# Moving the tiles that TensorE reads: gaps of 32 to 384 bytes around the split weights, combined x and summed quarters

## The chip, the cores and the metric

The kernel runs on one core of a Trainium2 chip. The metric is the device time of one launch in microseconds (us), lower is better. The time before is the median of three runs: 3024.18 us (3021.7 to 3024.24).

## The reference, cut to what matters

The reference is a stack of two blocks over a sequence of 512 tokens with a width of 1024, all in float32. The first block has two layers, each with a fused input projection, retention, a state-space scan, forgetting attention and an output projection. The second has two layers, each of which is

```
x = layer_norm(ALPHA * x + 0.5 * swiglu(x, wg[0], wu[0], wd[0]))
x = layer_norm(ALPHA * x + token_mix(x, w_in, w_out, ...))
x = layer_norm(ALPHA * x + 0.5 * swiglu(x, wg[1], wu[1], wd[1]))
swiglu(x, wg, wu, wd) = (silu(x @ wg) * (x @ wu)) @ wd      # 1024 -> 2816 -> 1024
```

So there are four feed-forward halves, and beside them a row of projections from 1024 features.

## The kernel before, in words

**Products in two parts.** Every large product is made from operands that are split into a high part, rounded to float32r, and a low part, the rest. Three passes are added up in PSUM: high times high, high times low, low times high. A tile whose name ends in `_parts` holds both. Each matmul has a stationary operand of 128 x 128 (a weight load, PEld in the profile, goes ahead of the matmul) and a moving operand of 128 x 256 or 128 x 512. TensorE can load the next weights while the current matmul still streams.

**Tiles.** In each partition the persistent tiles lie in the order of their allocation, each at the next multiple of 32 bytes: `x_all`, `x_parts` (32,768 bytes, the activations), `w_raw`, `w_parts` (32,768 bytes: two slots, each with a high and a low part of 8,192 bytes), `cst` (3,796), `spec` (8,208), `par` (624), and behind them the tiles of the stages. In a feed-forward half these are `ffn_buffers`, `x_combined_parts` (32,768), `partial_parts` (8,192, two slots), `hidden_parts` (24,576) and `sum_parts` (24,576, two slots). Counted from the start of a partition, `x_parts` starts at byte 17,536, `w_parts` at 66,688, `x_combined_parts` at 137,280, `partial_parts` at 170,048, `hidden_parts` at 178,240 and `sum_parts` at 202,816.

**Weight units.** SP loads a unit of 8,192 bytes a partition into one of two slots of `w_raw`; ACT or DVE rounds it into the high part of the slot of `w_parts`, Pool or DVE makes the low part. In the projections this is `Stream` (`round`, `lower`), with the products in `Project` (L423 token by token, L347 and L425 with the weights as the moving operand). In the feed-forward halves it is `FeedForward.build`.

**A feed-forward half** goes through four `tile` units (L2212, moving 512 columns of `x_parts`), sixteen `quad` units, two more `tile` units and four `final` ones (L2293, moving `hidden_parts`; the last of them with 256 columns at L2304). A quad unit computes a 2 x 2 block product with seven multiplications (Winograd's form of Strassen's scheme), each 12 matmuls of 256 columns at L2250, in this order: a11 (`x_parts` against `w_parts`), s2 (`x_combined_parts` against `sum_parts`), s1 (`x_combined_parts` against `w_parts`), s3 (`x_combined_parts` against `sum_parts`), a12 (`x_parts` against `w_parts`), a22 (`x_combined_parts` against `w_parts`), s4 (`x_parts` against `sum_parts`). Behind s1 and behind a12 stands a partial product of the down projection (L2232: 12 matmuls of 512 columns, `hidden_parts` against `partial_parts`). Quads alternate: even ones are for the gate, odd ones for the up projection.

**The order of the work** is written out by hand on each engine. In a quad unit DVE does, in program order: the last combination of the quad before (L2542), the sums of the next unit's quarters (L2494 to L2501), one combination (L2523), the low part of the next unit (L2506), the low part of its sums (L2512), the addition of a partial product (L2555), and then L2528, for which PE waits ahead of a22:

```
pe.wait_ge(self.combined, 5 * q + 2)
multiply(a22, n4, 1, False)
```

Of the kernel before, what the change touches and what calls it, by code (L numbers as in the profile page):

```python
# [22 lines left out]
F32R = mybir.dt.float32r  # L23
# [5 lines left out]
T = 512  # L29
# [5 lines left out]
UNIT = KD * UC  # L35
SLOTS = 2
LOWERED = 512
HALF_TILE = P // 2
BIG = 1.0e30
EPS = 1e-6  # L40
LN_EPS = 1e-5
# [37 lines left out]
def split3(ap, a):  # L79
    return ap.rearrange("p (a b) -> p a b", a=a)  # L80
# [7 lines left out]
def repeat(ap, n):  # L88

    return ap.unsqueeze(1).broadcast_to([ap.shape[0], n, ap.shape[1]])  # L90


class Stream:
# [63 lines left out]
def build(nc, dr, out):  # L157
    ctx = ExitStack()
    with ctx:
        named = Counter()  # L160

        def sb(name, n, dt=F32, stack=None):
            named[name] += 1
            return (stack or ctx).enter_context(nc.sbuf_tensor(f"{name}{named[name] if named[name] > 1 else ''}", [P, n], dt))
# [53 lines left out]
        x_all = sb("x_all", KD * T)  # L218
        xs_all = sb("x_parts", 2 * KD * T, F32R)
        w_raw = sb("w_raw", SLOTS * UNIT)  # L220
        w_parts = sb("w_parts", 2 * SLOTS * UNIT, F32R)
        cst = sb("cst", C0N)
        spec = sb("spec", CN)
        par = sb("par", P1N)
        X = split3(x_all[:, :], KD)
        XS = xs_all[:, :].rearrange("p (a k t) -> p a k t", a=2, k=KD)
        RAW = split3(w_raw[:, :], SLOTS)
        WP = w_parts[:, :].rearrange("p (s a n) -> p s a n", s=SLOTS, a=2)
        ident = cst[:, 0:128]
        ones = cst[:, 128:256]  # L230
        triu = cst[:, 256:384]
# [49 lines left out]
        class Project:  # L281
# [20 lines left out]
            def both_parts(self, source):  # L302


                u = self.stream.add(source, KD * HALF_TILE, self.projected, len(self.jobs) + 1, turns=True)
                self.jobs.append((u, "b", 0, P, HALF_TILE, KD))
                return len(self.jobs) - 1
# [24 lines left out]
            def run_half(self, pe, j):  # L332
# [7 lines left out]
                if not second:  # L340
                    if self.jobs[j - c - 1][1] == "second":
                        pe.wait_ge(self.evacuated, j - c - 2 * NT + 2 * (c + 1))
                    elif c < 2:
                        pe.wait_ge(self.evacuated, j - 1)
                w = [WP[:, self.stream.slot(u), a, :].rearrange("p (k n) -> p k n", k=kt) for a in range(2)]
                def product(k, a, b, start, stop):
                    return pe.matmul(PS[:, self.bank(j), 0:m], XS[:, a, kt * second + k, c * P:(c + 1) * P], w[b][:, k, :],  # L347
                                     start=start and not second, stop=stop and second)
# [14 lines left out]
            def begin(self, pe, jobs, x, order=range(KD), between=None):  # L363
# [4 lines left out]
                for n in range(KD + 1):  # L368
                    if between and n in between:
                        between[n]()  # L370
                    if n < KD:
                        k = order[n]
                        pe.wait_ge(x.high, n + 1)
                        for j in jobs:
# [3 lines left out]
                            for a in range(2):  # L378
                                w = WP[:, self.stream.slot(u), a, 0:kt * ncols].rearrange("p (k n) -> p k n", k=kt)
                                pe.matmul(PS[0:m, self.bank(j), :], w[:, k, c:c + m], XS[:, 0, k, :],  # L380
                                          start=(n == 0 and a == 0), stop=False)
                    if n:
                        k = order[n - 1]
                        pe.wait_ge(x.low, n)
                        for j in jobs:
                            u, kind, c, m, ncols, kt = self.jobs[j]
                            w = WP[:, self.stream.slot(u), 0, 0:kt * ncols].rearrange("p (k n) -> p k n", k=kt)
                            last = pe.matmul(PS[0:m, self.bank(j), :], w[:, k, c:c + m], XS[:, 1, k, :],  # L388
# [4 lines left out]
            def run(self, pe, j, part, between=None):  # L393
# [16 lines left out]
                if kind == "b":  # L410
                    w = WP[:, self.stream.slot(u), 0, 0:kt * m].rearrange("p (k n) -> p k n", k=kt)
                    for k in range(kt):
# [6 lines left out]
                    return  # L419
                w = [WP[:, self.stream.slot(u), a, 0:kt * ncols].rearrange("p (k n) -> p k n", k=kt) for a in range(2)]  # L420
                def product(k, w_, x_, start, stop):
                    if kind == "f":
                        return pe.matmul(PS[0:m, self.bank(j), :], w[w_][:, k, c:c + m], part(x_, k),  # L423
                                         start=start, stop=stop)
                    return pe.matmul(PS[:, j % 2, 0:m], part(x_, k)[:, c * P:(c + 1) * P], w[w_][:, k, :],  # L425
                                     start=start, stop=stop)
# [16 lines left out]
            def after(self, j, act):  # L443

                u = self.jobs[j][0] if j >= 0 else -1
                if j + 1 == len(self.jobs) or self.jobs[j + 1][0] != u:
                    self.stream.round(act, act.copy, RAW, WP, u + 1 + SLOTS)

# [253 lines left out]
        first = ExitStack()  # L702
# [432 lines left out]
        def scan_and_attend(block, l, streams, norm, after):  # L1135
# [451 lines left out]
            def _(dve):  # L1587
# [6 lines left out]
                for h in range(2):  # L1594
                    norm_retention(h)
                dve.wait_ge(s_dt, 1)
                link(dve.tensor_tensor(dtf, split3(PS[:, 7, 0:96], NT), repeat(p1("dtf_b"), NT), ALU.add))
                dve.scalar_tensor_tensor(mag, dtf, -1.0, dtf, ALU.mult, ALU.max).then_inc(s_ab, 1)
                dve.wait_ge(s_ex, 1)
# [11 lines left out]
                                         ALU.min, ALU.subtract).then_inc(s_lf, 1)  # L1611
                dve.wait_ge(s_al, 1)
                dve.scalar_tensor_tensor(aa, dtf[:, :, 0:16], -1.0, repeat(amat, NT),
                                         ALU.mult, ALU.mult).then_inc(s_a, 1)

# [370 lines left out]
        HALF, QUARTER = T // 2, KD // 2 * P  # L1986
        SMALL = EARLY * P
# [10 lines left out]
        class FeedForward:  # L1998
# [78 lines left out]
            def build(self, block, before, after):  # L2077
                half, slot = self.half, self.slot
                ar = Arena(f"ffn{half}", 4 * T + 6 * HALF + 3 * QUARTER + 2 * SMALL)
# [2 lines left out]
                flat_sums = ar.take(3 * QUARTER)  # L2082
                sums = split3(flat_sums, 3)
                small_raw = split3(ar.take(2 * SMALL), 2)
                xt = ar.parts(f"x_combined_parts{half}", 8 * 4 * HALF).rearrange("p (a n k t) -> p a n k t", a=2, n=4, k=4)
                small_parts = ar.parts(f"partial_parts{half}", 4 * SMALL).rearrange("p (s a n) -> p s a n", s=2, a=2)
                hidden = ar.parts(f"hidden_parts{half}", 6 * 2 * T).rearrange("p (k a t) -> p k a t", k=6, a=2)
                early = ExitStack()
                xc = sb(f"x_combined{half}", 4 * 4 * HALF, stack=early)[:, :].rearrange("p (n k t) -> p n k t", n=4, k=4)
                early.close()  # L2090
                more = ar.parts(f"sum_parts{half}", 2 * 2 * 3 * QUARTER).rearrange("p (s a n) -> p s a n", s=2, a=2)
                ln = self.norm(f"ffn{half}_norm")
                passes = ((0, 0), (0, 1), (1, 0))
                units = range(NU)
# [1469 lines left out]
def constants():  # L3564
# [6 lines left out]
    c0[:, 256:384] = i[:, None] <= i[None, :]  # L3571
    c0[:, 768:896] = np.where(i[None, :] > i[:, None], -BIG, 0.0)
    c0[:, 896] = (10000.0 ** (-(i % 64) / 64.0)).astype(f)
# [19 lines left out]
    for q in range(NT):  # L3593
        ok = (np.arange(32)[None, :] * CS + CB - 1 <= (q * P + i)[:, None]) & (np.arange(32) < NCMP)[None, :]
        c2[:, 1536 + 32 * q:1568 + 32 * q] = np.where(ok, 0.0, -BIG)
        c2[:, 1664 + 32 * q:1696 + 32 * q] = ok
# [9 lines left out]
def layout(a):  # L3606

    def units(w, cols, n):

        L, K, _ = w.shape  # L3610
        w = w[:, :, cols].reshape(L, K // P, P, len(cols) // n, n)
        return np.ascontiguousarray(w.transpose(0, 3, 2, 1, 4)).reshape(L, len(cols) // n, P, -1)

    def padded(w, cols):

        w = np.concatenate([w[:, :, cols], np.zeros((DEPTH, D, HALF_TILE - len(cols)), np.float32)], axis=2)
        return units(w, np.arange(HALF_TILE), HALF_TILE)[:, 0]

# [88 lines left out]
```

## Time and profile before

| | |
|---|---|
| median of three runs | 3024.18 us |
| the profiled execution, first to last instruction (its span) | 3021.6 us |
| PE busy | 2964.2 us, 98% |
| weight loads (PEld) busy | 2512.2 us, 83% |
| DVE, ACT, POOL busy | 1899.1, 1289.1, 1072.1 us |
| mean granted TensorE clock | 0.990 |

The profile gives the profiled execution's time as its span alone; the lowest of the three timed runs, 3021.7 us, is as long. Times in the profile are in microseconds from the start of the span unless marked ns. PE is TensorE's matmuls, PEld its weight loads. Matmuls are pipelined, so that the duration of one reaches over the start of the next: how fast they run is seen from the distance of their starts. `L423` is line 423 of the kernel.

### The profile page before, as it was taken

Reading aid. Unit: us, or ns where it says so; the run is one execution under the profiler, and the core shown is the slowest. Engines: PE = TensorE matmul, PEld = TensorE weight load, DVE = VectorE, ACT = ScalarE, POOL = GpSimd, SP = SyncE. Lnnn points to the kernel's source line nnn. Section 1 sums busy time; section 2 is a strip of 40 time slices with the busy share of each in tenths; the row PEclk is TensorE's granted clock in tenths of the full one; section 3 lists DMA queues with packets and bytes.
Section 4 is the critical chain, followed back from the end, with each engine's and each line's share of the span. In section 5 each row is a group of like instructions: output and inputs, shape, how many; then the busy total and the mean of one; then the engine's idle time right before and its main releaser. Section 6 shows DMA issues by size and latency. Waiting matters only on the chain. (4 is left out here: it accounts for less than half of the span.)

```text
span 3021.6 us, 43644 instructions
## 1 busy us (share of the span) xinstructions
PE 2964.2 (98%) x17620; PEld 2512.2 (83%) x17620; DVE 1899.1 (63%) x2758; ACT 1289.1 (43%) x2015; POOL 1072.1 (35%) x786
## 2 busy tenths in 40 slices
PE   8999999999999999999999999999999999999998
PEld 6887878788778799988767899988998776789996
DVE  8476245747524377855386778657785537677875
ACT  4356442436553243424463534334343346453432
POOL 2443445535353422225342322242222534132222
PEclk8999999999999999999999999999999999999999
DMA  6223315313231233322110323223332221033321
GB/s 275 101 85 112 101 51 198 138 59 127 83 122 37 88 114 105 105 85 89 67 43 29 111 99 105 98 78 118 102 103 83 92 70 43 29 105 105 102 101 49
DMA packets 57440, 287.61 MB, mean 95 GB/s; under 512 B 6777, under 2 KB 7289, under 8 KB 30201
## 3 DMA queue, kind: packets, MB, share of 16 engines
q1 hardware_dynamic: 54000, 269.30, 25.3%
q10 hardware_dynamic: 3240, 15.53, 1.6%
q8 instruction: 140, 2.29, 0.3%
q14 instruction: 60, 0.48, 0.1%
HBM read 282.64 MB, written 2.16 MB: 94 GB/s over the span
## 5 line engine op out<-in xcount | busy, mean ns | idle before, releaser
L152 POOL TENSOR_TENSOR w_parts<-w_raw,w_parts 128x512 fp32r<-128x512 f32 x376 | 537.7, 1460 | 687.0 <-ACT w_parts L141 664.3
L423 PE MATMUL PS<-x_parts,w_parts 128*128 128x512 f32 x2640 | 655.1, 394 | 1.6 <-ACT m_all L1430 1.6
L423 PEld LDWEIGHTS PS<-x_parts,w_parts 128*128 128x128 f32 x2640 | 490.7, 188 | 111.3 <-issue 9.6
L2191 POOL TENSOR_TENSOR partial_parts<-ffn_buffers,partial_parts 128x512 fp32r<-128x512 f32 x128 | 183.0, 1431 | 747.6 <-ACT partial_parts L2398 747.6
L2232 PE MATMUL PS<-hidden_parts,partial_parts 128*128 128x512 f32 x1536 | 372.7, 391 | 0.0
L2232 PEld LDWEIGHTS PS<-hidden_parts,partial_parts 128*128 128x128 f32 x1536 | 280.1, 188 | 53.3
L2212 PE MATMUL PS<-x_parts,w_parts 128*128 128x512 f32 x1152 | 265.9, 392 | 3.1 <-POOL x_parts L1977 3.1
L2212 PEld LDWEIGHTS PS<-x_parts,w_parts 128*128 128x128 f32 x1152 | 215.9, 188 | 52.1 <-POOL x_parts L1977 4.5
L141 ACT CAST w_parts<-w_raw 128x2048 fp32r<-128x2048 f32 (+1 forms) x92 | 170.6, 1854 | 163.1 <-PE PS L423 73.8
L2250 PE MATMUL PS<-x_parts,w_parts 128*128 128x256 f32 x1536 | 204.3, 282 | 0.0
L2250 PE MATMUL PS<-x_combined_parts,w_parts 128*128 128x256 f32 x1536 | 204.0, 282 | 0.0
L2250 PE MATMUL PS<-x_combined_parts,sum_parts 128*128 128x256 f32 x1536 | 203.0, 281 | 0.0
L2250 PEld LDWEIGHTS PS<-x_combined_parts,sum_parts 128*128 128x128 f32 x1536 | 195.9, 190 | 5.0
L2250 PEld LDWEIGHTS PS<-x_combined_parts,w_parts 128*128 128x128 f32 x1536 | 191.6, 189 | 10.1 <-DVE ffn_buffers L2528 7.4
L2398 ACT CAST partial_parts<-ffn_buffers 128x512 fp32r<-128x512 f32 x128 | 79.2, 621 | 270.5 <-PE PS L2232 270.5
L2250 PEld LDWEIGHTS PS<-x_parts,w_parts 128*128 128x128 f32 x1536 | 192.4, 190 | 0.3
L347 PE MATMUL PS<-w_parts,x_parts 128*128 128x512 f32 x768 | 185.4, 399 | 1.4 <-ACT ssd_buffers L1468 1.4
L347 PEld LDWEIGHTS PS<-w_parts,x_parts 128*128 128x128 f32 x768 | 143.8, 188 | 38.3 <-issue 7.2
L2388 ACT CAST w_parts<-w_raw 128x2048 fp32r<-128x2048 f32 x64 | 122.5, 1915 | 88.2 <-DVE w_raw L2496 87.4
L2506 DVE TENSOR_TENSOR w_parts<-w_raw,w_parts 128x2048 fp32r<-128x2048 f32 x64 | 146.7, 2292 | 17.4 <-ACT w_parts L2388 17.4
L2378 ACT CAST hidden_parts<-ffn_buffers 128x512 fp32r<-128x512 f32 x88 | 54.6, 621 | 220.0 <-DVE ffn_buffers L2548 119.2
L2512 DVE TENSOR_TENSOR sum_parts<-ffn_buffers,sum_parts 128x1536 fp32r<-128x1536 f32 x64 | 148.3, 2318 | 0.0
(445 smaller groups left out, 5008.0 us busy)
## 6 DMA issues: line engine op xcount, KB each, us to landing
w_raw<-in_w_gu SPq DMA_DIRECT2D x88, 1024.0 KB, 4.8
w_raw<-in_w_in SPq DMA_DIRECT2D x70, 1024.0 KB, 4.9
ffn_buffers<-in_w_part SPq DMA_DIRECT2D x128, 256.0 KB, 2.7
w_raw<-in_w_out SPq DMA_DIRECT2D x24, 1024.0 KB, 4.8
m_all<-in_w_next SPq DMA_DIRECT2D x14, 1024.0 KB, 7.7
w_raw<-in_w_last SPq DMA_DIRECT2D x12, 768.0 KB, 4.1
m_all<-in_w_gate SPq DMA_DIRECT2D x8, 1024.0 KB, 5.0
ssd_buffers<-decay_rows ACTq DMA_DIRECT2D x16, 512.0 KB, 4.0
```

The source lines that it names most:

```text
L141: op(self.part(parts, u, 0, 0, n), raw[:, self.slot(u), 0:n]).then_inc(self.high, 1)
L152: pool.tensor_tensor(self.part(parts, u, 1, at, to), raw[:, self.slot(u), at:to], self.part(parts, u, 0, at, to).bitcast(F32), ALU.subtrac ...
L347: return pe.matmul(PS[:, self.bank(j), 0:m], XS[:, a, kt * second + k, c * P:(c + 1) * P], w[b][:, k, :], start=start and not second, stop ...
L423: return pe.matmul(PS[0:m, self.bank(j), :], w[w_][:, k, c:c + m], part(x_, k), start=start, stop=stop)
L2191: pool.tensor_tensor(small_parts[:, d % 2, 1, :], small_raw[:, d % 2, :], small_parts[:, d % 2, 0, :].bitcast(F32), ALU.subtract).then_inc ...
L2212: return pe.matmul(PS[:, 2 * b + g, :], WP[:, slot(b), w, c:c + P], XS[:, x, k, :], start=start, stop=stop)
L2232: last = pe.matmul(PS[:, 6 + d % 2, :], small_parts[:, d % 2, w, k * P:(k + 1) * P], hid(x, EARLY * c + k), start=(i == j == 0), stop=(i = ...
L2250: last = pe.matmul(bank(q, n), w(wa, k), x(xa, k), start=(first and k == 0 and i == 0), stop=(k == 3 and i == 2), skip_group_check=True)
L2388: act.copy(WP[:, b, 0, :], RAW[:, b, :]).then_inc(self.wide, 1)
L2398: act.copy(small_parts[:, d % 2, 0, :], small_raw[:, d % 2, :]).then_inc(self.small_high, 1)
L2506: dve.tensor_tensor(WP[:, b, 1, :], RAW[:, b, :], WP[:, b, 0, :].bitcast(F32), ALU.subtract).then_inc(self.sums, 1)
L2512: dve.tensor_tensor(split3(more[:, b, 1, :], 3), sums, split3(more[:, b, 0, :], 3).bitcast(F32), ALU.subtract).then_inc(self.sums, 1)
```

## The change

`w_parts` is allocated with 96 elements (384 bytes) ahead of its first slot and 48 elements (192 bytes) behind each slot. `x_combined_parts` begins 8 elements (32 bytes) later in its tile, `partial_parts` has 16 elements (64 bytes) behind each of its slots, and `sum_parts` 40 elements (160 bytes) behind each; `hidden_parts` has no gap. The larger tiles move what is allocated behind them: everything behind `w_parts` starts 768 bytes later, `partial_parts` 800, `hidden_parts` and `sum_parts` 928. `x_parts` and what lies before it stay. No instruction, wait or order changes.

```diff
+FIRST_GAP, SLOT_GAP = 96, 48
+PART_GAPS = dict(x_combined=(8, 0), partial=(0, 16), hidden=(0, 0), sums=(0, 40))
...
+def slots_of(ap, gap, n):
+
+    return ap.rearrange("p (s r) -> p s r", s=2)[:, :, 0:n].rearrange("p s (a n) -> p s a n", a=2)
...
-        w_parts = sb("w_parts", 2 * SLOTS * UNIT, F32R)
+        w_parts = sb("w_parts", FIRST_GAP + SLOTS * (2 * UNIT + SLOT_GAP), F32R)
...
-        WP = w_parts[:, :].rearrange("p (s a n) -> p s a n", s=SLOTS, a=2)
+        WP = slots_of(w_parts[:, FIRST_GAP:], SLOT_GAP, 2 * UNIT)
...
-                xt = ar.parts(f"x_combined_parts{half}", 8 * 4 * HALF).rearrange("p (a n k t) -> p a n k t", a=2, n=4, k=4)
-                small_parts = ar.parts(f"partial_parts{half}", 4 * SMALL).rearrange("p (s a n) -> p s a n", s=2, a=2)
-                hidden = ar.parts(f"hidden_parts{half}", 6 * 2 * T).rearrange("p (k a t) -> p k a t", k=6, a=2)
+                def parts_behind_gap(name, n):
+                    first, between = PART_GAPS[name]
+                    return ar.parts(f"{name}_parts{half}", first + n + 2 * between)[:, first:], between
+
+                xt = parts_behind_gap("x_combined", 8 * 4 * HALF)[0].rearrange("p (a n k t) -> p a n k t", a=2, n=4, k=4)
+                small_parts = slots_of(*parts_behind_gap("partial", 4 * SMALL), 2 * SMALL)
+                hidden = parts_behind_gap("hidden", 6 * 2 * T)[0].rearrange("p (k a t) -> p k a t", k=6, a=2)
...
-                more = ar.parts(f"sum_parts{half}", 2 * 2 * 3 * QUARTER).rearrange("p (s a n) -> p s a n", s=2, a=2)
+                more = slots_of(*parts_behind_gap("sums", 2 * 2 * 3 * QUARTER), 2 * 3 * QUARTER)
```

## Rows read from the trace of the kernel before

**Rows 1.** The page's part 1: busy us, share of the span, instructions, by engine.

```profile
PE 2964.2 (98%) x17620; PEld 2512.2 (83%) x17620; DVE 1899.1 (63%) x2758; ACT 1289.1 (43%) x2015; POOL 1072.1 (35%) x786
```

**Rows 2.** Span and mean granted TensorE clock of the core.

```profile
core 0: 3021.6 us, clock 0.990
```

**Rows 3.** PE groups by form: count, busy us, mean ns; idle before, releaser.

```profile
L423 PE MATMUL PS<-x_parts,w_parts 128*128 128x512 f32 x2640 | 655.1, 394 | 1.6 <-ACT m_all L1430 1.6
L2232 PE MATMUL PS<-hidden_parts,partial_parts 128*128 128x512 f32 x1536 | 372.7, 391 | 0.0
L2212 PE MATMUL PS<-x_parts,w_parts 128*128 128x512 f32 x1152 | 265.9, 392 | 3.1 <-POOL x_parts L1977 3.1
L2250 PE MATMUL PS<-x_parts,w_parts 128*128 128x256 f32 x1536 | 204.3, 282 | 0.0
...
L347 PE MATMUL PS<-w_parts,x_parts 128*128 128x512 f32 x768 | 185.4, 399 | 1.4 <-ACT ssd_buffers L1468 1.4
L2293 PE MATMUL PS<-hidden_parts,w_parts 128*128 128x512 f32 x432 | 103.8, 399 | 0.0
L425 PE MATMUL PS<-w_parts,x_parts 128*128 128x256 f32 x768 | 101.2, 291 | 1.6 <-POOL w_parts L152 1.4
...
L2304 PE MATMUL PS<-hidden_parts,sum_parts 128*128 128x256 f32 x144 | 17.9, 283 | 0.0
```

**Rows 4.** Timeline of PE, 50 to 190: start, length, group, count.

```profile
53.85 54.56 PE L423 MATMUL PS<-x_parts,w_parts 128*128 128x512 f32 x240
108.25 23.19 PE L425 MATMUL PS<-w_parts,x_parts 128*128 128x256 f32 x192
131.28 0.82 PE L1016 MATMUL PS<-cst,retention_buffers 128*128 128x128 f32 x6
```

**Rows 5.** Timeline of PE in the final units of a half, 1350 to 1392.

```profile
1350.75 12.76 PE L2293 MATMUL PS<-hidden_parts,w_parts 128*128 128x512 f32 x54
1363.35 1.02 PE L1804 MATMUL PS<-x_all,cst 128*128 128x512 f32 x2
...
1381.74 4.48 PE L2304 MATMUL PS<-hidden_parts,sum_parts 128*128 128x256 f32 x36
1386.06 0.95 PE L1814 MATMUL PS<-cst,ffn_buffers 128*128 128x1 f32 x8
```

**Rows 6.** Timeline of PE: a first quad's a22; an even and an odd quad.

```profile
1094.14 1.58 PE L2250 MATMUL PS<-x_combined_parts,w_parts 128*128 128x256 f32 x12
...
1143.34 1.59 PE L2250 MATMUL PS<-x_parts,w_parts 128*128 128x256 f32 x12
...
1155.96 1.67 PE L2250 MATMUL PS<-x_combined_parts,w_parts 128*128 128x256 f32 x12
1157.47 1.53 PE L2250 MATMUL PS<-x_parts,sum_parts 128*128 128x256 f32 x12
1158.83 1.60 PE L2250 MATMUL PS<-x_parts,w_parts 128*128 128x256 f32 x12
1160.27 1.58 PE L2250 MATMUL PS<-x_combined_parts,sum_parts 128*128 128x256 f32 x12
...
1171.46 1.58 PE L2250 MATMUL PS<-x_combined_parts,w_parts 128*128 128x256 f32 x12
1172.87 1.58 PE L2250 MATMUL PS<-x_parts,sum_parts 128*128 128x256 f32 x12
1174.29 1.60 PE L2250 MATMUL PS<-x_parts,w_parts 128*128 128x256 f32 x12
```

**Rows 7.** Timeline of DVE in the same quads: the chain's head, and L2528.

```profile
1093.14 0.41 DVE L2528 TENSOR_TENSOR ffn_buffers<-PS,ffn_buffers 128x256 f32<-128x256 f32 x1
...
1143.54 0.42 DVE L2542 TENSOR_TENSOR ffn_buffers<-ffn_buffers,PS 128x256 f32<-128x256 f32 x1 [0.19 <-PE PS L2250]
...
1155.50 0.41 DVE L2528 TENSOR_TENSOR ffn_buffers<-PS,ffn_buffers 128x256 f32<-128x256 f32 x1
...
1167.48 0.42 DVE L2528 TENSOR_TENSOR ffn_buffers<-PS,ffn_buffers 128x256 f32<-128x256 f32 x1
```

## The prediction

> **What bounds the kernel now.** I read the busy shares first. TensorE (PE) is busy 2964.2 of 3021.6 us, 98%, DVE 63%, ACT 43% [rows 1], and its granted clock averages 0.990 of the 2.4 GHz level [rows 2]. So nearly all of the time is matmuls in a row, and what counts is how far apart their starts are. The change touches no instruction, no wait, no queue and no shape: it only moves tiles. It can act on the time only if the start-to-start distance of matmuls depends on where their two operands lie.
>
> The mean durations of the groups [rows 3] don't show that, because a matmul is pipelined and its duration (some 282 ns for 256 columns, 391 to 399 ns for 512) overlaps the next. The timeline does: take the start of one run, the start of the next, and divide by the count.
> - 512 columns, x_parts against w_parts: (108.25 - 53.85) / 240 = 226.7 ns [rows 4].
> - 256 columns, w_parts against x_parts: (131.28 - 108.25) / 192 = 119.9 ns [rows 4].
> - 512 columns, hidden_parts against w_parts: (1363.35 - 1350.75) / 54 = 233.3 ns, with no idle time shown [rows 5].
> - 256 columns, hidden_parts against sum_parts: (1386.06 - 1381.74) / 36 = 120.0 ns [rows 5].
> - 256 columns inside the quad units: x_parts/w_parts (1160.27 - 1158.83) / 12 = 120 ns; x_parts/sum_parts once (1158.83 - 1157.47) / 12 = 113.3 ns and once (1174.29 - 1172.87) / 12 = 118.3 ns [rows 6].
>
> So one shape has two or three speeds, and the slow one of 512 columns has other tiles than the fast one. The lowest, 113.3 and 226.7, I call the floor. The last pair has the same tiles at two speeds: the fast one stands behind a matmul run that began with a wait, so how the weight load and the moving read stand to each other in time matters beside the address.
>
> The distance in bytes from the moving tile to the stationary one, modulo 512 (the step between two 128-column weight blocks), follows from the order of allocation and the sizes. Before: x_parts/w_parts 0; x_combined/sum_parts 0; hidden/partial 0; hidden/sum_parts 0; x_combined/w_parts 64; hidden/w_parts 64; x_parts/sum_parts 448 (64 the other way). With rows: at distance 0 the 256-column form is at its slowest (120), the 512-column one at the floor; at 64 the 512-column form is slow (233.3); at 448 the 256-column form has 118.3 or 113.3.
>
> **The change, part by part.** After it the distances (slot 0, slot 1) are: x_parts/w_parts 384, 64 (576); x_combined/w_parts 160, 352; x_combined/sum_parts 128, 288; x_parts/sum_parts 352, 0; hidden/partial 384, 448; hidden/w_parts 32, 224; hidden/sum_parts 0, 160. Nearly every pair leaves its old distance, and no row shows what most of the new ones cost. So each form is bounded from both sides by the rows of its shape.
>
> (a) Quad units, 84 matmuls of 256 columns and 24 of 512 each; 64 units, 16 in each of four feed-forward halves (1536 + 1536 + 1536 + 768 matmuls of L2250 and 1536 of L2232; the first group and L2232 stand in [rows 3]). An odd unit lasts 1174.29 - 1158.83 = 15.46 us [rows 6]; at the floor 84 x 0.1133 + 24 x 0.2267 = 14.96. Bounds for an odd unit: 0.50 us saved, or, with all 256-column matmuls at 120 (now 118.7 on average: (15.46 - 24 x 0.2287) / 84, with 228.7 for the 512s, halfway between floor and what two steps above it would give), 0.11 lost. I take the middle between 113.3 and 120, 116.7, as both ends are seen at the present distances and the new ones lie between: 84 x 2.0 ns = 0.17, and 0.02 for the 512s: 0.19 us a unit.
>
> What hides it: in an even unit the a22 products wait for DVE. L2528 ends at 1155.50 + 0.41 = 1155.91 and they start at 1155.96; the DVE work before it began at 1143.54, 0.20 behind the unit's start at 1143.34, and is a chain of its own [rows 6, 7]. A PE that is faster in the first 60 + 24 matmuls arrives earlier and waits longer; behind the wait it runs at 113.3 already. So even units give nothing (7 of 8; 28 in all). In an odd unit L2528 ends at 1167.90 against a start of a22 at 1171.46, 3.56 us of room; in the first unit of a half 1093.55 against 1094.14, 0.59 [rows 6, 7], more than the 0.36 that a floor-fast first part could save. So 32 odd and 4 first units count: 36 x 0.19 = 6.8 us (bounds: -4 to +18).
>
> (b) The other 256-column forms, L425 768 and L2304 144 [rows 3], from 119.9 to 116.7: 912 x 3.3 ns = 3.0 us (bounds 0 to 6.0).
>
> (c) L2293, 432 matmuls at 233.3 [rows 3, 5], distance 64 to 32 and 224: halfway to the floor, 432 x 3.3 = 1.4 us (0 to 2.9).
>
> (d) The 512-column x_parts/w_parts forms: L423 2640, L2212 1152, L347 768, together 4560 [rows 3], at the floor [rows 4]. They can't gain. I take 0; the other end is the 6.6 ns of L2293: 30 us lost. I take 0 because the slow 512-column row has w_parts, too, but a moving tile that starts 64 bytes off a 128-byte boundary, while x_parts stays where it is, on one; that is weak, and is the first rival.
>
> (e) Everything behind w_parts moves by 768 bytes or more (constants, buffers, par). ACT, DVE and Pool work on them, and have room (63% and less) except in the even units, where DVE's 12.4 us chain sets the a22 start. I take its durations as unchanged; 1% on it would be 0.12 x 28 = 3.5 us either way. DMA sizes and issues are the same: nothing.
>
> Sum: 6.8 + 3.0 + 1.4 = 11.2 us, made against the profiled execution's span of 3021.6. The median of the runs is 3024.18, 2.6 us above the span (0.09%); I put the saving under the median: 3024.2 - 11.2 = 3013.
>
> The Trainium skill, "SBUF — State Buffer", section "Who interferes with whom", says that PE has two SBUF read ports, one for the moving operand and one for the weight load, and never waits on anyone; by this rule no address could matter and the time would stay at 3024. The trace disagrees with it in this kernel: 226.7 against 233.3 ns for one shape with no wait shown [rows 4, 5].
>
> **The rivals.**
> 1. Slower: the 512-column forms leave the one distance at which they are known to be at the floor. Slot 1 of w_parts gets distance 64 to x_parts, the very distance of the 233.3 ns row [rows 5]. Half of 4560 times 6.6 ns = 15.0 us lost, against 11.2 gained: 3028. With slot 0 as bad: 3043. It decides from 11.2 / 4560 = 2.5 ns a matmul on. For it: the only slow 512-column row is the one at a distance of 64. Against it: at 64 and 448 the 256-column forms are faster than at 0, and L2293's moving tile is another.
> 2. Large gain: the new distances keep all forms at the floor, as x_parts/sum_parts at 1157.47 [rows 6]. 36 x 0.50 + 6.0 + 2.9 = 27 us: 2997. Against it: the same pair is at 118.3 in the unit beside.
> 3. No change: the speeds come from the rhythm of the instruction pairs (the entry behind a wait), not the address; all shifts are multiples of 32 bytes. 3024. For it: 113.3 and 118.3 at one distance [rows 6]. Against it: 226.7 against 233.3.
>
> **How the numbers follow.** Forecast 0.47, large gain 0.16, no change 0.13, slower 0.24. A difference under 0.2%, 6 us, can't be told from none. Faster: 0.16 + 0.46 (0.01 of the forecast's chance lies within 6 us) = 0.62; same 0.14; slower 0.24. The range is 2994 to 3034: it takes in the large gain and the milder slower case, with the 3.5 us of (e) on either side and a little for the pricing of rival 1, and leaves out both slots slow (3043). The likeliest case alone has 3004 to 3018.
>
> **What would show it.** Right: the run of L425 (192 matmuls in 23.03 us) gets shorter, towards 22.4; the run of L423 (240 in 54.40) stays; odd units fall below 15.46 and even ones stay near 15.49 with L2528's end still just before a22. Slower rival: L423's run grows beyond 55.0. Large gain: L425's run at 21.8 and odd units at 15.0. No change: every one of these stays. The prediction is wrong if L423 moves, or if even units shorten (then DVE's chain was not the limit).

## The result, and the profile after

The changed kernel takes 3046.2 us (median of 4 runs, 3042.4 to 3047.5) where the kernel before takes 3023.8 us (4 runs, 3021.7 to 3024.2). The ratio is 1.0075, 95% interval 1.006 to 1.009: slower by 0.75%, or 22 us. The forecast was 3013 us, faster by 11 us; the time also lies outside the range of 2994 to 3034.

The page of the profile after, its head and part 1 (busy us, share, instructions by engine), and under it the core's span and clock:

```profile
span 3045.3 us, 43644 instructions
PE 2989.2 (98%) x17620; PEld 2512.0 (82%) x17620; DVE 1899.2 (62%) x2758; ACT 1288.1 (42%) x2015; POOL 1066.9 (35%) x786
```

```profile
core 0: 3045.3 us, clock 0.991
```

The span grew by 23.7 us, PE's busy time by 25.0, with the same 17620 matmuls; DVE and ACT have what they had, Pool 5 us less, and the clock is 0.991 for 0.990 [rows 1, 2]. So the loss is in how closely the matmuls follow one another. Line numbers are 7 to 11 higher than before (L423 is now L430, L425 L432, L347 L354, L2212 L2223, L2232 L2243, L2250 L2261, L2293 L2304, L2304 L2315, L2528 L2539), and the tile `sum_parts` is called `sums_parts`.

PE groups by form after: count, busy us, mean ns, idle before. They answer to [rows 3]:

```profile
L430 PE MATMUL PS<-x_parts,w_parts 128*128 128x512 f32 x2640 | 666.7, 398 | 1.6 <-ACT m_all L1437 1.6
L2243 PE MATMUL PS<-hidden_parts,partial_parts 128*128 128x512 f32 x1536 | 376.1, 393 | 0.0
L2223 PE MATMUL PS<-x_parts,w_parts 128*128 128x512 f32 x1152 | 271.9, 396 | 4.3 <-POOL x_parts L1984 3.5 <-POOL x_parts L873 0.7
L2261 PE MATMUL PS<-x_parts,w_parts 128*128 128x256 f32 x1536 | 199.8, 279 | 0.0
...
L354 PE MATMUL PS<-w_parts,x_parts 128*128 128x512 f32 x768 | 187.9, 402 | 1.3 <-ACT ssd_buffers L1475 1.3
L2304 PE MATMUL PS<-hidden_parts,w_parts 128*128 128x512 f32 x432 | 103.8, 399 | 0.0
L432 PE MATMUL PS<-w_parts,x_parts 128*128 128x256 f32 x768 | 97.3, 284 | 1.5 <-POOL w_parts L159 1.5
```

The 512-column forms lose: 655.1 to 666.7, 265.9 to 271.9, 372.7 to 376.1, 185.4 to 187.9. The 256-column forms with `w_parts` and `x_parts` gain: 204.3 to 199.8 and 101.2 to 97.3. Busy time counts the union of overlapping instructions, so I also summed the start-to-start distances over all matmuls of either trace: `x_parts`/`w_parts` in 512 columns +21.1 us, `w_parts`/`x_parts` in 512 columns +2.3, `hidden_parts`/`partial_parts` +4.8, `x_combined_parts`/`w_parts` +1.1, `x_parts`/`sums_parts` +1.4, the matmuls of unsplit float32 +1.4; the 256-column `x_parts`/`w_parts` -4.6 and `w_parts`/`x_parts` -3.9. That is 23.6 of the span's 23.7.

Only about 1 us of the last term is speed. The rest is two stretches of the token-mixing stage in which the 24 matmuls stood further apart before. Timeline of PE in one of them, before, and then in e1_parts_only, the first experiment below, whose distance for this pair is as before:

```profile
2413.86 4.64 PE L425 MATMUL PS<-w_parts,x_parts 128*128 128x256 f32 x24
2418.34 0.97 PE L2831 MATMUL PS<-cst,mixer_buffers 112*128 112x24 f32 x8
```

```profile
2420.08 3.13 PE L432 MATMUL PS<-w_parts,x_parts 128*128 128x256 f32 x24
2423.04 0.97 PE L2842 MATMUL PS<-cst,mixer_buffers 112*128 112x24 f32 x8
```

The 24 matmuls take 4.48 us before and 2.96 in e1 (and 2.96 in the changed kernel). In all, the pair's matmuls lose 3.0 us in e1 too, so these 3 us don't come from the pair's distance. What held them apart isn't shown.

Timeline of PE after, the runs of [rows 4] and [rows 5]: start, length, group, count:

```profile
54.59 56.06 PE L430 MATMUL PS<-x_parts,w_parts 128*128 128x512 f32 x240
110.49 22.87 PE L432 MATMUL PS<-w_parts,x_parts 128*128 128x256 f32 x192
133.19 0.82 PE L1023 MATMUL PS<-cst,retention_buffers 128*128 128x128 f32 x6
...
1362.53 12.76 PE L2304 MATMUL PS<-hidden_parts,w_parts 128*128 128x512 f32 x54
1375.12 1.02 PE L1811 MATMUL PS<-x_all,cst 128*128 128x512 f32 x2
```

The run of 240 takes 110.49 - 54.59 = 55.90 us, 232.9 ns a matmul, where it took 54.40, 226.7 ns: the forecast's own sign of the slower rival ("beyond 55.0"). The run of 192 takes 22.70 us, 118.2 ns, from 119.9. The run of 54 takes 12.59, from 12.60: unchanged at 233.1 ns.

Timeline of PE after, an even and an odd quad unit, for [rows 6]; then DVE's L2539, the last thing that a22 waits for, for [rows 7]:

```profile
1154.46 1.58 PE L2261 MATMUL PS<-x_parts,w_parts 128*128 128x256 f32 x12
...
1167.12 1.60 PE L2261 MATMUL PS<-x_combined_parts,w_parts 128*128 128x256 f32 x12
1168.56 1.57 PE L2261 MATMUL PS<-x_parts,sums_parts 128*128 128x256 f32 x12
1169.97 1.52 PE L2261 MATMUL PS<-x_parts,w_parts 128*128 128x256 f32 x12
1171.33 1.58 PE L2261 MATMUL PS<-x_combined_parts,sums_parts 128*128 128x256 f32 x12
...
1185.33 1.58 PE L2261 MATMUL PS<-x_parts,w_parts 128*128 128x256 f32 x12
```

```profile
1166.32 0.41 DVE L2539 TENSOR_TENSOR ffn_buffers<-PS,ffn_buffers 128x256 f32<-128x256 f32 x1
...
1178.56 0.42 DVE L2539 TENSOR_TENSOR ffn_buffers<-PS,ffn_buffers 128x256 f32<-128x256 f32 x1
```

The even unit takes 15.51 us, the odd one 15.36. In this even unit a22 starts 0.39 us behind L2539's end (1166.73), so here PE itself comes late; in 3 of the 28 even units that aren't the first of a half the gap is 0.40, in 11 some 0.1, in 14 0.06, where all 28 had 0.06 before. Over all four halves even units average 15.565 us (15.480 before), odd ones 15.453 (15.459 before).

### The profile page after: what moved, and what is told of

It reads as the page before. It is cut to its first block and busy times, and to the rows that moved or that the text cites. A ratio compares the mean times of both kernels' runs of the same rounds, so it can differ in the third digit from the quotient of the medians.

```text
span 3045.3 us, 43644 instructions
## 1 busy us (share of the span) xinstructions
PE 2989.2 (98%) x17620; PEld 2512.0 (82%) x17620; DVE 1899.2 (62%) x2758; ACT 1288.1 (42%) x2015; POOL 1066.9 (35%) x786
## 5 line engine op out<-in xcount | busy, mean ns | idle before, releaser
L430 PE MATMUL PS<-x_parts,w_parts 128*128 128x512 f32 x2640 | 666.7, 398 | 1.6 <-ACT m_all L1437 1.6
L430 PEld LDWEIGHTS PS<-x_parts,w_parts 128*128 128x128 f32 x2640 | 491.4, 188 | 121.7 <-issue 9.6
L2243 PE MATMUL PS<-hidden_parts,partial_parts 128*128 128x512 f32 x1536 | 376.1, 393 | 0.0
L2243 PEld LDWEIGHTS PS<-hidden_parts,partial_parts 128*128 128x128 f32 x1536 | 280.0, 188 | 55.3
L2223 PE MATMUL PS<-x_parts,w_parts 128*128 128x512 f32 x1152 | 271.9, 396 | 4.3 <-POOL x_parts L1984 3.5
L2223 PEld LDWEIGHTS PS<-x_parts,w_parts 128*128 128x128 f32 x1152 | 215.7, 188 | 59.3 <-POOL x_parts L1984 4.3
L2261 PE MATMUL PS<-x_combined_parts,w_parts 128*128 128x256 f32 x1536 | 204.9, 282 | 0.0
L2261 PE MATMUL PS<-x_combined_parts,sums_parts 128*128 128x256 f32 x1536 | 202.6, 281 | 0.0
L2261 PEld LDWEIGHTS PS<-x_combined_parts,w_parts 128*128 128x128 f32 x1536 | 193.2, 188 | 11.2 <-DVE ffn_buffers L2539 7.8
L2261 PE MATMUL PS<-x_parts,w_parts 128*128 128x256 f32 x1536 | 199.8, 279 | 0.0
L2261 PEld LDWEIGHTS PS<-x_combined_parts,sums_parts 128*128 128x128 f32 x1536 | 195.1, 188 | 5.5
L354 PE MATMUL PS<-w_parts,x_parts 128*128 128x512 f32 x768 | 187.9, 402 | 1.3 <-ACT ssd_buffers L1475 1.3
L2261 PEld LDWEIGHTS PS<-x_parts,w_parts 128*128 128x128 f32 x1536 | 188.7, 188 | 0.3
L354 PEld LDWEIGHTS PS<-w_parts,x_parts 128*128 128x128 f32 x768 | 144.1, 188 | 40.5 <-issue 7.2
L2523 DVE TENSOR_TENSOR sums_parts<-ffn_buffers,sums_parts 128x1536 fp32r<-128x1536 f32 x64 | 148.4, 2318 | 0.0
```

Of the source, the lines that this page charges most:

```text
L2223: return pe.matmul(PS[:, 2 * b + g, :], WP[:, slot(b), w, c:c + P], XS[:, x, k, :], start=start, stop=stop)
L2243: last = pe.matmul(PS[:, 6 + d % 2, :], small_parts[:, d % 2, w, k * P:(k + 1) * P], hid(x, EARLY * c + k), start=(i == j == 0), stop=(i = ...
L2261: last = pe.matmul(bank(q, n), w(wa, k), x(xa, k), start=(first and k == 0 and i == 0), stop=(k == 3 and i == 2), skip_group_check=True)
L2523: dve.tensor_tensor(split3(more[:, b, 1, :], 3), sums, split3(more[:, b, 0, :], 3).bitcast(F32), ALU.subtract).then_inc(self.sums, 1)
```

## The experiments

All are edits of the changed kernel's constants unless a longer diff stands. "Distance" is the bytes from the moving to the stationary tile, modulo 512, as in the prediction. The 1.0 of each ratio is the kernel before, measured beside the runs (3023.3 us beside the e runs, 3024.2 beside the f runs, 3023.2 beside the g runs).

### Halves of the change: the tiles behind, or w_parts

e1_parts_only keeps the gaps of the three feed-forward tiles and takes those of `w_parts` away:

```diff
-FIRST_GAP, SLOT_GAP = 96, 48
+FIRST_GAP, SLOT_GAP = 0, 0
```

> Theory D (the speed of a matmul goes by the distance from the moving to the stationary tile modulo 512; the 512-column form has its floor of 226.7 ns only at 0): w_parts back at distance 0 to x_parts brings the 512-column forms of x_parts and w_parts back to 226.7 (the run of 240 back to 54.40 us); hidden_parts against partial_parts keeps 384 and 448 and stays at about 232 and 230. About 3024 + 5 = 3029 us (3025 to 3032). Rival Q (the gaps inside the quad units carry the loss): stays near 3040 or above. Rival A (not the distance but the moved addresses of what lies behind w_parts, worked on by DVE, ACT and Pool): 160 to 480 bytes remain, some loss spread over all engines, 3030 to 3046, with DVE and ACT groups of longer mean duration.

e2_w_only is the other half:

```diff
-PART_GAPS = dict(x_combined=(8, 0), partial=(0, 16), hidden=(0, 0), sums=(0, 40))
+PART_GAPS = dict(x_combined=(0, 0), partial=(0, 0), hidden=(0, 0), sums=(0, 0))
```

> Theory D: the 512-column forms of x_parts and w_parts at distance 384 and 64 take about 232 to 233 ns, some 23 us more than before; the 256-column x_parts/w_parts and w_parts/x_parts forms gain about 8 us; hidden_parts against partial_parts is back at distance 0: 3038 to 3042 us. Rival Q: about 3024, as the quad tiles are not moved against each other. Rival A: 3046, as everything behind w_parts is moved by 768 bytes as in the changed kernel.

Measured: e1 3026.4 us, ratio 1.0012 [1.0003, 1.0022]; e2 3041.5 us, 1.006 [1.0045, 1.0075]. Timeline of PE, first e1, then e2:

```profile
57.42 54.56 PE L430 MATMUL PS<-x_parts,w_parts 128*128 128x512 f32 x240
111.82 23.19 PE L432 MATMUL PS<-w_parts,x_parts 128*128 128x256 f32 x192
134.85 0.82 PE L1023 MATMUL PS<-cst,retention_buffers 128*128 128x128 f32 x6
```

```profile
54.53 56.07 PE L430 MATMUL PS<-x_parts,w_parts 128*128 128x512 f32 x240
110.44 22.87 PE L432 MATMUL PS<-w_parts,x_parts 128*128 128x256 f32 x192
133.14 0.82 PE L1023 MATMUL PS<-cst,retention_buffers 128*128 128x128 f32 x6
```

In e1 both runs are those of before to 0.01 us (54.40, 23.03); in e2 both are those of after (55.91, 22.70). So the move of `w_parts` makes both, and costs about 18 us. The other gaps cost about 3: in e1 the group `hidden_parts`/`partial_parts`, which left distance 0 for 384 and 448, is busy 375.7 us against 372.7 [rows 3], and in e2, where both tiles moved together, 372.0.

### Is it the distance, and modulo what?

e3_first512 moves `w_parts` and all behind it by 512 bytes; e4_first64 by 64:

```diff
-FIRST_GAP, SLOT_GAP = 96, 48
+FIRST_GAP, SLOT_GAP = 128, 0
```

> Only a first gap of 512 bytes: w_parts and everything behind it moves by 512 bytes, and every distance modulo 512 is as before. Theory D: each form keeps its speed and the time is that of before, 3024 us within 0.1%. Rival A (moved addresses cost by themselves): slower, 3035 to 3046. If the distance counts modulo more than 512 (1024 or 2048), the run of 240 moves away from 54.40 us.

```diff
-FIRST_GAP, SLOT_GAP = 96, 48
+FIRST_GAP, SLOT_GAP = 16, 0
```

> Only a first gap of 64 bytes: x_parts/w_parts goes from distance 0 to 64 in both slots, x_parts/sum_parts from 448 to 0, all other distances stay. Theory D: 512-column x_parts/w_parts 233 ns instead of 226.7 (the run of 240: 55.9 us), about 5040 matmuls, +30 us; the 256-column x_parts/w_parts matmuls of the quads fall from 119.7 to about 114.5, -4 us where PE sets the time, and w_parts/x_parts at L432 to 117.8, -2 us: 3046 to 3050 us. Rival A: a move of 64 bytes costs a twelfth of 768: within 0.1% of 3024.

(Both also have PART_GAPS at zero, as in e2.) Measured: e3 3023.6 us, ratio 1.0000 [0.9991, 1.001]; e4 3041.7 us, 1.006 [1.0045, 1.0075]. Timeline of PE in e3, then in e4:

```profile
53.76 54.56 PE L430 MATMUL PS<-x_parts,w_parts 128*128 128x512 f32 x240
108.16 23.19 PE L432 MATMUL PS<-w_parts,x_parts 128*128 128x256 f32 x192
131.19 0.82 PE L1023 MATMUL PS<-cst,retention_buffers 128*128 128x128 f32 x6
```

```profile
53.80 56.16 PE L430 MATMUL PS<-x_parts,w_parts 128*128 128x512 f32 x240
109.80 22.77 PE L432 MATMUL PS<-w_parts,x_parts 128*128 128x256 f32 x192
132.41 0.82 PE L1023 MATMUL PS<-cst,retention_buffers 128*128 128x128 f32 x6
```

e3 moves everything that the change moves and leaves every distance as it was modulo 512: no effect. So a move of the constants, buffers or weights costs nothing by itself, and it is not a distance modulo more than 512. A shorter period isn't excluded. At distances 256 apart the 512-column matmuls are equally fast (128 and 384: 232.5 and 232.5 ns; 192 and 448: 229.1 and 229.5; 160 and 416: 233.5 and 233.4), so that modulo 256 fits these rows as well; modulo 128 doesn't (64 and 192: 233.3 and 229.1).

e4 leaves the pairs behind `w_parts` to each other as they were, gives `x_parts`/`w_parts` 64 and takes `x_parts`/`sums_parts` from 448 to 0: 56.00 us for the run of 240 (233.3 ns), 22.61 for the run of 192 (117.8). The 233.3 is what I expected; the whole came 4 us or more below what I expected. The sums of the start-to-start distances say why: the 512-column matmuls with `x_parts` and `w_parts` lost 24.6 us and not 30 (23.1 as `x_parts`/`w_parts`, 5.4 ns each, and 1.4 as `w_parts`/`x_parts`, which lies at 448 when the other way round is 64, and has 229.6 ns there). The 256-column forms gained 4.7 us together, 3 of them in the two stretches of the token-mixing stage.

### The other direction: 512 columns to distance 0, 256 columns off it

If that is the rule, tiles can be placed by it. f1_hidden64 leaves `w_parts` alone and starts `partial_parts` and what lies behind it 64 bytes later. That brings `hidden_parts`/`w_parts` from 64 to 0, `x_combined_parts`/`sums_parts` from 0 to 64, `x_parts`/`sums_parts` from 448 to 0, and leaves `hidden_parts`/`partial_parts` at 0 and `x_combined_parts`/`w_parts` at 64:

```diff
-FIRST_GAP, SLOT_GAP = 96, 48
-PART_GAPS = dict(x_combined=(8, 0), partial=(0, 16), hidden=(0, 0), sums=(0, 40))
+FIRST_GAP, SLOT_GAP = 0, 0
+PART_GAPS = dict(x_combined=(0, 0), partial=(16, 0), hidden=(0, 0), sums=(0, 0))
```

> w_parts without gaps, partial_parts, hidden_parts and sum_parts 64 bytes later: every 512-column pair is at distance 0 (hidden_parts/w_parts comes from 64 to 0), x_combined/sum_parts goes to 64, x_parts/sum_parts to 0. Theory D (distance modulo 512 sets the speed, 512 columns want 0): the run of 54 at L2304 falls from 12.60 to 12.24 us (226.7 ns), 432 x 6.6 ns = 2.9 us saved, x_parts/sum_parts at 120 costs up to 2 us, x_combined/sum_parts between 113.3 and 117.7: 3019 to 3023 us. Rival B (the last tile's speed goes by its place on a 128-byte boundary, not by the distance): hidden_parts is now on a 128-byte boundary as well, so this run alone can't tell B from D for it; B expects x_combined/sum_parts, whose moving tile stays off the boundary, to stay at 118.5.

Measured: 3016.5 us, ratio 0.9975 [0.9965, 0.9985], faster than the 3019 to 3023 that I expected. Timeline of PE in f1, the run of 54 of [rows 5]:

```profile
1351.23 12.40 PE L2304 MATMUL PS<-hidden_parts,w_parts 128*128 128x512 f32 x54
1363.47 1.02 PE L1811 MATMUL PS<-x_all,cst 128*128 128x512 f32 x2
```

12.24 us, 226.7 ns: the form that took 230 to 234 ns in every kernel up to here is at the floor as soon as its distance is 0, with the same tiles and the same instructions. It gives 2.6 us (the group's busy time 103.8 to 101.2), and `x_combined_parts`/`sums_parts` 3.5 (203.0 to 199.5). `x_combined_parts`/`w_parts` gives 3.7 (204.0 to 200.3) although its distance of 64 is unchanged: behind s2 it now steps at 113.3 ns, where it had 117.8, and no wait stands ahead. `x_parts`/`sums_parts` loses 2.3 (99.6 to 101.9).

One tile can't lie at 0 for the 512-column forms and elsewhere for the 256-column ones, so f3_split gives the quads' weights their own offset in the slot of `w_parts`, 64 bytes in, and places the rest so that all 256-column pairs of the quads have distance 64 and all 512-column pairs 0, except the 72 matmuls of `hidden_parts`/`sums_parts`, which get 64 (233.3 ns):

```diff
+FIRST_GAP, SLOT_GAP = 0, 128
+QUAD_SHIFT, TOKEN_SHIFT = 16, 112
+PART_GAPS = dict(x_combined=(16, 0), partial=(0, 0), hidden=(0, 0), sums=(16, 0))
...
+        WQ = w_shifted(QUAD_SHIFT)
...
-                        act.copy(WP[:, b, 0, :], RAW[:, b, :]).then_inc(self.wide, 1)
+                        act.copy(WQ[:, b, 0, :], RAW[:, b, :]).then_inc(self.wide, 1)
```

(DVE's low part and PE's `kept_quarters` read and write `WQ` in the same way; `w_shifted(n)` is the view of the two slots from element n on.)

> The quad units write and read their weights 64 bytes further in the slot than all other units; x_combined, partial_parts and hidden_parts 64 bytes later, sum_parts 128. So all 256-column pairs of the quads are at distance 64 and all 512-column pairs at 0 (hidden/sum_parts at 64). Theory D: 512-column forms at their floor, quads at 113.3 to 117.7 ns; an odd quad unit between 15.0 and 15.35 us instead of 15.46, even ones near 15.49 (DVE's chain holds them); 36 x 0.1 to 0.45 us + 2.9 us = 3005 to 3018 us. Rival P (inside a distance the rhythm decides, 117.7 is the lock unless a wait stands before): 3015 to 3018.

f4_quad_only is f3 without the gaps of the other tiles (PART_GAPS zero): only the quads' weights move, by 64 bytes.

> Only the quad units' weights lie 64 bytes further in their slot, all tiles else keep their distances: x_parts/w_parts in the quads 64, x_combined/w_parts 128, x_combined/sum_parts 0, x_parts/sum_parts 448. Theory D: 512-column forms unchanged; of the quads' pairs one better (64), one worse (128, 118.5 to 119): 3019 to 3024 us, worse than f3_split by at least 4 us. Rival P (x_parts/w_parts decides alone, as in slot 1 of the changed kernel): as fast as f3_split without its 2.9 us.

f5_split_tokens is f3 with the units of the 256-column projections (L425 before) moved in their slot as well, by 448 bytes, which brings their distance from 0 to 64:

```diff
-        WQ = w_shifted(QUAD_SHIFT)
+        WQ, WT = w_shifted(QUAD_SHIFT), w_shifted(TOKEN_SHIFT)
...
+                self.stream.shifted[u] = WT
```

> f3_split, and the units whose weights are the moving operand of 256 columns at L432 lie 448 bytes further in their slot, which puts x_parts at distance 64 from them instead of 0. Theory D, with 64 as the good distance for 256 columns: the run of 192 falls from 23.03 us to 21.8 to 22.6; 768 matmuls, 2 to 5 us below f3_split. Rival B (the boundary of 128 bytes): the moving tile is off the boundary now, so no gain.

g3_split192 is f3 with 192 in place of 64 for all four 256-column pairs of the quads:

```diff
-QUAD_SHIFT, TOKEN_SHIFT = 16, 112
-PART_GAPS = dict(x_combined=(16, 0), partial=(0, 0), hidden=(0, 0), sums=(16, 0))
+QUAD_SHIFT, TOKEN_SHIFT = 48, 112
+PART_GAPS = dict(x_combined=(16, 0), partial=(0, 0), hidden=(0, 0), sums=(48, 0))
```

> f3_split with distance 192 instead of 64 for all 256-column pairs of the quads. Theory D in its strict form (64 is the good distance, all others but 0 are alike at 118 to 119): odd units 15.43 instead of 15.33, 3018 to 3021 us. Rival (192 is as good or better, as x_combined/w_parts at 192 had 115.4 in e2_w_only): odd units at or below 15.33, 3012 to 3017 us.

| | median us | ratio [95%] | odd units, us | even units, us |
|---|---|---|---|---|
| before | 3023.8 | 1 | 15.459 | 15.480 |
| after | 3046.2 | 1.0075 [1.006, 1.009] | 15.453 | 15.565 |
| f1 | 3016.5 | 0.9975 [0.9965, 0.9985] | 15.353 | 15.527 |
| f3 | 3016.7 | 0.9975 [0.9965, 0.9985] | 15.328 | 15.518 |
| f4 | 3023.1 | 0.9996 [0.9987, 1.0004] | 15.373 | 15.572 |
| f5 | 3012.9 | 0.9963 [0.9951, 0.9976] | 15.322 | 15.511 |
| g3 | 3015.4 | 0.9977 [0.9967, 0.9987] | 15.316 | 15.525 |

f5 against f3 changes one pair only, 768 matmuls. The medians are 3.8 us apart, with intervals that overlap; by the traces 2.1 us of it are this pair's, and the rest lies in groups that the step doesn't touch. PE's timeline in f5 has

```profile
53.39 54.56 PE L438 MATMUL PS<-x_parts,w_parts 128*128 128x512 f32 x240
107.79 22.78 PE L440 MATMUL PS<-w_parts,x_parts 128*128 128x256 f32 x192
130.41 0.82 PE L1031 MATMUL PS<-cst,retention_buffers 128*128 128x128 f32 x6
```

22.62 us for the run of 192 (117.8 ns) and 54.40 for the run of 240: the gain of the change at L425 without its loss at L423. f4, where only the quads' weights moved (`x_parts`/`w_parts` 64, `x_combined_parts`/`w_parts` 128, the other pairs as before), gives nothing that can be told: its odd units gain 0.09 us, its even ones lose as much. f3 came out at the slow end of what I expected, and no faster than f1: its 256-column forms go mostly at 117.8 ns, not at the floor, although `x_parts`/`w_parts` at the same distance of 64 goes at 114.1 in f4. g3 refutes my expectation that only 64 is good: at 192 the quads are as fast as at 64 (the intervals overlap). f5 beats the kernel before by 0.37% and the changed one by 33 us; only g1, which is f5 with one more step, is level with it.

### The wait for DVE in even units

The last two experiments move no tile. g1_split_order is f5 with one step of DVE's program order moved in even quads: the addition of the first partial product goes behind `lower_right` and the combination that a22 waits for. g2_order_only does the same to the kernel before.

```diff
-                        if beside:
+                        late = q is not None and q % 2 == 0
+                        if beside and not late:
...
+                            if beside and late:
+                                add_partial(beside[0])
```

> f5_split_tokens, and in even quad units DVE does the combination that a22 waits for ahead of the addition of the partial product (0.68 us), not behind it. Theory C (DVE's chain is what keeps the even units from gaining by faster matmuls): its end moves 0.7 us ahead, the wait before a22 goes, even units fall from 15.51 us to the 15.32 of the odd ones: 28 x 0.19 = 5.3 us, 3006 to 3009 us. Rival (something else holds the even units, or the wait's good rhythm of 113.3 ns behind it is worth as much as the wait costs): even units stay at 15.5 and the time near 3013.

> The same change of DVE's order without any shift (all distances as before). Theory C: the wait of some 100 ns ahead of a22 goes, but the 24 matmuls behind it then run at 118 instead of 113.3, which costs 0.11 us: even units 15.46 instead of 15.48, 0.5 us in all, 3023 to 3024 us. So the gain of g1 below f5 has to come from the distances and the order together. Rival (the order is worth its 0.1 us by itself in 28 units, or more): 3020 to 3021.

Measured: g1 3012.7 us, ratio 0.9966 [0.9954, 0.9978], where I expected 3006 to 3009; g2 3022.2 us, 0.9996 [0.9987, 1.0005]. The wait is gone, the gain isn't there. Timeline of PE in f5, an even unit's a22 and the odd unit behind it, then of DVE's combination (L2547 here) ahead of that a22:

```profile
1120.86 2.91 PE L2251 MATMUL PS<-hidden_parts,partial_parts 128*128 128x512 f32 x12
1123.67 1.65 PE L2269 MATMUL PS<-x_combined_parts,w_parts 128*128 128x256 f32 x12
1125.16 1.52 PE L2269 MATMUL PS<-x_parts,sums_parts 128*128 128x256 f32 x12
1126.52 1.52 PE L2269 MATMUL PS<-x_parts,w_parts 128*128 128x256 f32 x12
1127.88 1.52 PE L2269 MATMUL PS<-x_combined_parts,sums_parts 128*128 128x256 f32 x12
1129.24 1.52 PE L2269 MATMUL PS<-x_combined_parts,w_parts 128*128 128x256 f32 x12
1130.60 2.91 PE L2251 MATMUL PS<-hidden_parts,partial_parts 128*128 128x512 f32 x12
1133.34 1.58 PE L2269 MATMUL PS<-x_combined_parts,sums_parts 128*128 128x256 f32 x12
1134.76 1.58 PE L2269 MATMUL PS<-x_parts,w_parts 128*128 128x256 f32 x12
```

```profile
1123.21 0.41 DVE L2547 TENSOR_TENSOR ffn_buffers<-PS,ffn_buffers 128x256 f32<-128x256 f32 x1
```

And PE in g1, with the combination in the same place of the chain:

```profile
1154.73 2.91 PE L2251 MATMUL PS<-hidden_parts,partial_parts 128*128 128x512 f32 x12
1157.48 1.58 PE L2269 MATMUL PS<-x_combined_parts,w_parts 128*128 128x256 f32 x12
1158.89 1.58 PE L2269 MATMUL PS<-x_parts,sums_parts 128*128 128x256 f32 x12
1160.30 1.58 PE L2269 MATMUL PS<-x_parts,w_parts 128*128 128x256 f32 x12
```

```profile
1156.48 0.41 DVE L2547 TENSOR_TENSOR ffn_buffers<-PS,ffn_buffers 128x256 f32<-128x256 f32 x1
```

In f5 a22 starts 0.05 us behind L2547's end and 2.81 us behind the 512-column product; in g1 0.59 us behind L2547's end and 2.75 behind the product, as where nothing waits. But behind f5's wait the matmuls step at (1126.52 - 1125.16) / 12 = 113.3 ns, through four products, until the next 512-column product; then they are at (1134.76 - 1133.34) / 12 = 118.3. In g1's quads no stretch of 113.3 is left: every unit, even and odd, lasts 15.387 us. In f5 odd units last 15.226 where the wait left them in the quick rhythm (about 4 in 10) and 15.384 elsewhere. Even units fell by 0.124 us on the average, odd ones rose by 0.065: 28 x 0.124 - 32 x 0.065 = 1.4 us, and the medians are the same. A wait on PE here costs its length and gives much of it back.

## Why the prediction was wrong

- **(d), the step that failed.** The 4560 matmuls of 512 columns with `x_parts` and `w_parts` were priced at 0 ("They can't gain. I take 0; the other end is ... 30 us lost"). They lost 20.5 us, 4.5 ns a matmul on the average, and 480 more matmuls of the same kind in smaller groups another 2.9: together the 23.4 us (21.1 + 2.3) above. In long runs the step is 6 ns and more in either slot, 233.3 ns at distance 64 and 232.5 at 384 for 226.7; the run of 240, which takes units from both, has 55.90 us for 54.40. The 768 with the weights moving lost 3.0 ns each. The prediction had the row that said so, the 233.3 ns at a distance of 64 [rows 5], and set it aside because the moving tile of that row is another one and starts off a 128-byte boundary while `x_parts` starts on one. e4 refutes that reason: it shows 233.3 for `x_parts` at distance 64, with `x_parts` on its 128-byte boundary as always. f1 can't tell the two apart, for there `hidden_parts` comes to distance 0 and onto a boundary at once; but in f4 `hidden_parts` is 64 bytes off one, and its first run of 12 against `partial_parts`, at distance 0, has 227.5 ns. What counts is the distance of the pair, not where the moving tile lies.
- **Rival 1** was the right mechanism. It gave 3028 with the slot at distance 64 bad and 3043 with the one at 384, which had no row, as bad; both are. That 3043 lies near the measured 3046.2 is partly luck: the loss of the 4560 was priced at 30 us and is 20.5, the gains at 11.2 and are 8.5 (4.6 + 3.9) with 3 us in them that no distance made, and 4.8 us of `hidden_parts`/`partial_parts` and 2.9 of the smaller groups weren't in it.
- **(a), -6.8 us.** Quads got slower by 2.5 us instead (928.1 to 930.6, all units but the last of each half). The forecast counted their 512-column product as slightly faster; at distances 384 and 448 it is slower (+4.8 us). Of the 256-column pairs only `x_parts`/`w_parts` gained clearly, 3.0 ns a matmul where I took 2.0 for every pair; `x_combined_parts`/`sums_parts` gained 0.2, and `x_combined_parts`/`w_parts` and `x_parts`/`sums_parts` lost 0.7 and 1.8. The cover was right: even units are held by DVE's chain, here too in 14 of 28 with 0.06 us between L2539's end and a22 (28 of 28 before); f1, f3, f4 and f5 shorten the odd units by 0.09 to 0.14 us and no even one.
- **(b), -3.0 us.** The direction is right, the size was a third of it: 22.70 us for the run of 192 (22.4 forecast), 119.9 to 118.2 ns, and L2304's 144 matmuls are unchanged. That is some 1 us; the -3.9 us in all fits the forecast by luck, for 3.0 of it stand in e1 as well, at distance 0.
- **(c), -1.4 us.** Wrong, and of the same kind as (d): distances 32 and 224 are as bad as 64 (12.59 us for 54; 233.2 and 233.3 ns). The speed isn't halfway because the distance is: of the distances tried, 192 and 448 lie between (229 to 230 ns).
- **(e), nothing.** Right as far as it was tried: DVE is busy 1899.2 us for 1899.1, ACT 1288.1 for 1289.1, and e3 moves everything by 512 bytes and gives 1.0000.
- **Rival 3**, only the rhythm and not the address, is refuted by e4 and f1, though rhythm is real (g1). **Rival 2** would have needed all forms at the floor: at best f5 reaches 3012.9 with tiles placed for it.

What stays open: why the distance matters. The runs say for which pairs and how much, and that a move by 512 bytes, the step between two weight blocks, changes nothing; they don't say whether the period is 512 or 256, nor whether the two reads share a resource and which. Nor was every distance tried. And for 256 columns the distance alone doesn't give the speed: what runs ahead counts as well (f1, f4 against f3).

## What to carry to other kernels

When PE is busy 98% and a change moves tiles, list for each pair of moving and stationary tile the distance modulo 512 before and after, and price each pair by a row of the same shape that left distance 0, before looking at what could gain. Here 512-column pairs belong at distance 0, and 256-column pairs at 64 or 192 (448 was as good), not at 0; where one tile serves both, give the units their own offsets in the slot (f5). And a row that is against the forecast outweighs a reason why it might not apply.

## What the runs showed of the hardware

The table has the mean start-to-start distance of matmuls that have the same pair, at the same distance, ahead and behind (steps of 250 ns and more for 512 columns, 140 and more for 256, left out as waits). A range spans the pairs and runs. "After" is the changed kernel.

| distance, bytes | 512 columns, ns | 256 columns, ns |
|---|---|---|
| 0 | 226.7 in long runs, 227.7 to 229.0 in `hidden_parts`/`partial_parts`, runs of 12 | 118.9 to 120.0 |
| 32 | 233.2 (after) | 118.6 (e1) |
| 64 | 233.2 to 233.4 (before, after, e2, e4, f3) | 114.1 to 117.8 |
| 96 | | 118.3 (e1) |
| 128 | 232.4 to 232.5 (after, e2) | 118.3 to 119.0 (after, e1, f4) |
| 160 | 233.4 to 233.6 (after, e1) | 119.3 to 120.0 (after, e1) |
| 192 | 229.0 to 229.1 (e2, g3) | 115.5 to 117.8 (e2, g3) |
| 224 | 233.3 (after) | |
| 256 | 228.2, but only 28 matmuls, 20 of them at 226 or 227 (after, e2) | 119.6 (e1) |
| 288 | | 118.1 to 118.2 (after, e1) |
| 352 | | 117.7 (after) |
| 384 | 232.5 to 232.8 (after, e1, e2) | 118.6 to 119.0 (after, e2) |
| 416 | 233.4 (e1) | |
| 448 | 228.9 to 230.0 (after, e1, e2, e4) | 115.8 to 118.1 (before, e3, e4, f4) |

- For 512 columns every distance with more than a few matmuls costs 2 to 7 ns against the 226.7 of distance 0, up to 3%. For 256 columns 0 is among the slowest, with 160 and 256, and 64, 192 and 448 are the fastest. So the best place for one shape is one of the worst for the other.
- At distance 64 there are two rhythms for 256 columns, 113.3 and 117.8 ns. A wait ahead can set the quick one, and it holds until the next 512-column product (f5, g1). It also comes without a wait: in f1 for s1 behind s2.
- The Trainium skill, "SBUF — State Buffer", section "Who interferes with whom", has PE never wait on anyone at its ports. In the run of 240 no matmul shows a wait, and yet the same pair of tiles takes 54.40 or 55.90 us: the measurement decides.
